# A fused diffusion layer kernel: six empty places in the order of the attention preparation, between the last tile's projections and its turned queries and keys

## The reference

```
q = (rmsnorm(q_c, qnorm_g) @ w_uq).reshape(B, L, MLA_H, QK_D)
return heads_first(with_rope(rmsnorm(q, q_g), rope))
...
k = jnp.concatenate([kv[..., :NOPE_D], broadcast(k_r)], axis=-1)
k = with_rope(rmsnorm(k, k_g), rope)
...
s = einsum('bhqd,bhkd->bhqk', q, k) * scale
o = einsum('bhqk,bhkd->bhqd', softmax(s), v)
```

## Time and profile before

| what | value |
|---|---|
| median of 3 runs | 1157.05 us (1155.04 to 1159.86) |
| the profiled execution's own time | 1148.31 us |
| its span in the profile | 1146.6 us |
| TensorE busy | 974.9 us, 85% of the span |
| VectorE busy | 451.5 us, 39% |
| ScalarE busy | 272.4 us, 24% |
| share of the chain that ended last | PE 73%, DVE 12%, issue 5% |

### The profile page before, as it was taken

How to read it: one execution, slowest core, us unless ns; L and a number is a source line. 1 busy time by engine, 2 the same in 40 slices (tenths; PEclk the granted TensorE clock), 3 DMA queues, 4 the chain that set the end, 5 groups by cost and what they waited for, 6 DMA issues and landing times.

```text
span 1146.6 us, 12445 instructions
## 1 busy us (share of the span) xinstructions
PE 974.9 (85%) x4417; PEld 537.2 (47%) x4417; DVE 451.5 (39%) x1149; ACT 272.4 (24%) x645; POOL 168.8 (15%) x204
## 2 busy tenths in 40 slices
PE   2799989979799995999999918998999698668872
PEld 0355444645476443755454404745655463433320
DVE  0305653667864245112121252266467732311103
ACT  0301213435443103021111111121436321111100
POOL 3350110201100001211212016002012000102000
PEclk8899989989999997999999968999899899889987
DMA  8962212577300009358888741522485033389973
GB/s 266 325 162 70 78 69 74 187 254 275 93 1 1 0 3 394 109 195 328 318 319 316 256 168 37 178 74 73 147 281 161 1 147 129 129 345 415 417 320 141
DMA packets 68442, 208.11 MB, mean 182 GB/s; under 512 B 10163, under 2 KB 18599, under 8 KB 59164
## 3 DMA queue, kind: packets, MB, share of 16 engines
q1 hardware_dynamic: 56416, 181.51, 42.9%
q0 software_dynamic: 9040, 16.25, 4.8%
q10 hardware_dynamic: 2924, 9.53, 2.2%
HBM read 199.99 MB, written 18.69 MB: 191 GB/s over the span
## 4 chain that ended last, share of the span: by engine, by line
PE 73%; DVE 12%; issue 5%; DMA 4%; POOL 2%; ACT 2%; ACTq 1%; SPq 0%; DVEq 0%; POOLq 0%
PE bank L1783 15%; PE bank L1701 8%; PE bank L1501 8%; PE bank L1489 8%; PE bank L1807 7%; PE bank L1411 7%; PE bank L1642 3%; PE bank L1575 3%; PE bank L1458 3%; POOL ST L1044 2%; PE bank L1553 2%; PE bank L1663 2%; PE bank L1759 2%; DMA BRANCH<-in_w_mod 1%; PE bank L1561 1%
## 5 line engine op out<-in xcount | busy, mean ns | idle before, releaser
L1783 PE MATMUL bank<-RINGW,NA 128*128 128x512 f32 (+1 forms) x448 | 176.9, 625 | 25.6 <-issue 23.2
L1783 PEld LDWEIGHTS bank<-RINGW,NA 128*128 128x128 f32 (+1 forms) x448 | 69.1, 174 | 126.4 <-issue 126.4
L1044 POOL TENSOR_TENSOR ST<-ST,RT 128x1 f32<-128x1 f32 (+4 forms) x46 | 51.4, 1117 | 502.3 <-DVE ST L1911 233.8
L1501 PE MATMUL bank<-RINGW,H 128*128 128x512 f32 (+4 forms) x384 | 119.0, 470 | 0.0
L2398 DVE SCALAR_TENSOR_TENSOR BRANCH<-BRANCH,bank 128x256 f32<-128x256 f32 x24 | 10.1, 421 | 237.9 <-ACT BRANCH L1355 237.9
L1489 PE MATMUL bank<-H,RINGW 128*96 128x512 f32 (+1 forms) x256 | 98.6, 543 | 4.0 <-ACT H L1158 2.7
L1701 PE MATMUL bank<-RINGW,H 128*128 128x512 f32 (+1 forms) x216 | 93.6, 593 | 0.0
L1501 PEld LDWEIGHTS bank<-RINGW,H 128*128 128x128 f32 x384 | 68.7, 190 | 49.4 <-issue 45.6
L1489 PEld LDWEIGHTS bank<-H,RINGW 128*96 128x96 f32 x256 | 41.6, 165 | 56.7 <-issue 51.9
L1701 PEld LDWEIGHTS bank<-RINGW,H 128*128 128x128 f32 (+1 forms) x216 | 40.6, 190 | 50.1 <-issue 50.0
L1411 PE MATMUL bank<-IDENT,WORK 128*128 128x128 f32 (+1 forms) x244 | 34.7, 291 | 34.3 <-DVE WORK L1913 33.2
(11 more groups left out here) (280 smaller groups left out, 1414.0 us busy)
## 6 DMA issues: line engine op xcount, KB each, us to landing
RINGW<-in_moe_w SPq DMA_DIRECT2D x56, 1024.0 KB, 11.3
RINGW<-in_w_mod SPq DMA_DIRECT2D x23, 2048.0 KB, 8.2
W2R<-in_moe_w SPq DMA_DIRECT2D x15, 1024.0 KB, 5.4
PROJ<-in_moe_w SPq DMA_DIRECT2D x11, 1024.0 KB, 16.8
WORK<-in_moe_w SPq DMA_DIRECT2D x8, 1024.0 KB, 18.6
RINGW<-in_w_in SPq DMA_DIRECT2D x4, 1536.0 KB, 8.3
RINGW<-in_w_out SPq DMA_DIRECT2D x4, 1536.0 KB, 10.7
RINGW<-in_w_in SPq DMA_DIRECT2D x2, 2048.0 KB, 9.4
```

The costliest lines, as they stand in the source:

```text
L1044: pool.tensor_tensor(r[:, 0:w], m[:, 0:w], POOL_HALF[:, 0:w], ALU.pow).then_inc(rstd_ready, 1)
L1501: ins = pe.matmul(bank_of(s)[:, 0:nn], HT[:, kk, t * P:(t + 1) * P], wv[:, kk, off:off + nn], start=kk == 0, stop=kk == KD - 1)
L1783: ins = pe.matmul(bank_of(s)[seats, :], XGT[n % 2][:, kk, seats], w[:, kk, :], start=kk == 0, stop=kk == KD - 1)
```

## The change

`prep` is given six entries `None` behind `uqn` of the last tile and ahead of its `qkT`. `merge` counts them as entries, so that units are set between them; then they are dropped. No step is added or removed, and no step's instructions change.

```
         prep = []
+        hold = [None] * 6
         for t in range(T + 1):
             now, last = t < T, t > 0
             prep += ([("cT", l, t)] if now else []) + ([("uqn", l, t - 1)] if last else [])
-            prep += ([("uqk", l, t)] if now else []) + ([("qkT", l, t - 1)] if last else [])
+            prep += ([("uqk", l, t)] if now else hold) + ([("qkT", l, t - 1)] if last else [])
             prep += [("uqs", l, t)] if now else []
...
-        s += spread(merge(prep, unit_steps(l, 1)), fill) + unit_steps(l, 0)
+        mixed = [x for x in merge(prep, unit_steps(l, 1)) if x]
+        s += spread(mixed, fill) + unit_steps(l, 0)
```

## The result

The changed kernel is slower: a median of 1163.82 us over 20 runs (1158.4 to 1168.74), against 1159.54 us for the kernel before over 20 runs on the same chips. The ratio is 1.0057, with a 95% interval of 1.0034 to 1.0081; it goes by the fast runs, without the three of the kernel before that lie over 1.5% above its fastest (1165.95, 1166.3 and 1376.84), and with only the last of them left out the means would give 1.0049. On the 1157.05 us of before that is +6.6 us, with an interval of +3.9 to +9.4. I had forecast +2.0 us and, with a chance of 0.62, a change too small to tell. The measured median lies inside the forecast range; the size of the change, which I had put at a third of what it is, is what failed, and in layer 1 a step of the mechanism with it.

What follows compares the result with a forecast made beforehand. TensorE, busy 85% of the span, was taken to bound the kernel, its late waits set by VectorE's in-order chain. Layer 0's -0.9 and layer 1's +2.9 us, added to 1157.05, gave 1159.0 us, range 1152 to 1166.

Steps and rivals of the forecast that it cites:

- What bounds the stage, and where the wait goes: Both layers: VectorE's in-order chain sets the end; waits move behind `uqn` 3, 2.9 us in layer 0, about 6 in layer 1.
- Layer 0, "-0.9 us": Layer 0: `uqn` 3 starts 4.5 us earlier, mostly spent on later waits; first scores at 319.5 against 320.43.
- the walk: Both layers: step-by-step timing of the new order on each engine, from measured durations and estimates for short steps.
- my bounds of -5.6 and +2.5: Layer 0: -5.6 us if the full 4.5 and 1.1 of clock come through, +2.5 if the clock is low at the end.
- Layer 1, "`uqn` 2 starts at 888.2, 0.8 us later": Layer 1: `qkT` 1, `mod` and `modT` ahead of `uqs` 2 on VectorE delay `uqn` 2 from 887.41 to 888.2 us.
- From `uqn` 2 to `uqn` 3, and from there to the scores: Layer 1: 11.4 to 12.5 us between them, before 12.3; `uqn` 3 ends 904.6 to 905.6, scores at 911.1 (909.0 to 912.2).
- The sum, "+2.0 us": Both layers: -0.9 and +2.9 us, total 1159.0 us, bounds -4.8 and +8.0; nothing behind the stages gives it back.
- less than 0.5% can't be told from no change: Whole kernel: a measurement can't resolve under 5.8 us; chances faster 0.14, within 0.62, slower 0.24.
- earlier preparation starves TensorE throughout: Rival, both layers: each `uqn` delays scores and `OM`s whose banks TensorE needs; three more waits, 9.8 us, 1167; chance 0.20.
- the places do what they seem to: Rival, both layers: both long waits vanish, as TensorE has more work beside `uqn` 3; -12.2 us, 1145; chance 0.14.
- The clock and transposes: Layer 0's tail: if transposes don't count as clock activity, some 2 us more, sum about +4; no chance changed.

Runs made afterwards that it cites:

- e4: Changed kernel with work TensorE needs (layer 0: reciprocal, `PV`, `OM`, two `S`; layer 1: `OM`, reciprocal) queued ahead of `uqn` 3; 1.0016 of the kernel before.
- e9: Kernel before plus, in layer 0 only, six places, reciprocals, `OM` and two scores ahead of `uqn` 3, `qkT` 3 and last `PV` behind four score tiles; ratio 0.9978.
- e1: Changed kernel with the six empty places in layer 0 only, layer 1 in the order of before; 1.0019 of the kernel before.
- e6: Changed kernel with matmuls nobody reads added in TensorE's long waits of both layers; 1.0028 of the kernel before.
- e3: Changed kernel with layer 1's two `mod` steps put back ahead of `uqk` 1 and `uqk` 2; 1.0087 of the kernel before.

## Why the prediction was off, point by point

- **What bounds the stage, and where the wait goes.** Right. The wait ahead of `qkT` 3 went in both layers. In layer 0 a wait for a reciprocal ahead of the `PV` sums came in its place (3.58 us, 2.9 forecast), in layer 1 a wait for an `OM` ahead of the last `PV` (6.42 us, about 6 forecast). e4 and e9 show that this queue behind `uqn` 3 is the cause: with it mended, the same places turn layer 0's loss of 1.9 us into gains of 1.8 and 4.1 us.
- **Layer 0, "-0.9 us".** The mechanism held and the term was mis-sized by 2.8 us, the larger part of the 4.2 us that the sum missed (e1 has it alone, 70.11 us against 68.25). `uqn` 3 started 54.8 us into the stage against 58.1 before, 3.3 us earlier where I had 4.5. From the end of `uqn` 3 to the first scores it was 10.4 us where I had 8.8: the walk ran the last transposes and `PV`s at full clock, and had the low one only in the bound. `ET` took 2.15 us and `PV` 1.98, both at low clock, and `qkT` 2.09, at low clock in its first part. That keeping TensorE busy there would have saved this isn't shown (e6 gained nothing in layer 0). +1.87 is within my bounds of -5.6 and +2.5.
- **Layer 1, "`uqn` 2 starts at 888.2, 0.8 us later".** This is the step whose mechanism failed. It started 3.05 us later. The walk had both long waits for `cT` and the `mod` that no longer covered them, but it had `uqk` 2 start 16.1 us into the stage and run at full clock. It started at 880.75 - 863.96 = 16.8, and the clock fell around that wait: `uqk` 2 lasted 1.8 us longer, `qkT`, `mod` and `modT` followed, and VectorE stood at `modT` for 2.95 us with `uqs` 2 behind it. I had named a low clock as a bound, and for the wrong tile (`uqk` 1, 1.5 us). e3 covers the waits, has `uqk` 2 at 2.21 us, and `uqn` 2 comes 4 us earlier. e6 leaves the order as it is, has `uqk` 2 at 2.21 us too, and `uqn` 2 comes 1.6 us earlier: that much of the 3.05 us is the clock's, the rest the order's.
- **From `uqn` 2 to `uqn` 3, and from there to the scores.** Right: 11.35 us (11.4 to 12.5 forecast), and 10.8 us from the start of `uqn` 3 to the scores (9.3 to 11.5 by my terms).
- **The sum, "+2.0 us".** Measured +6.2 in the stages and +6.6 in total; layer 0 missed by 2.8 us and layer 1 by 1.5, both towards slower. Nothing behind the stages gave it back, as said. That less than 0.5% can't be told from no change was too wide: the interval reaches 0.24% to each side. The forecast range of the total held the result because it was wide enough for both misses.
- **The rivals.** That earlier preparation starves TensorE throughout was the nearer one in kind: layer 1's new waits are such waits. But they wait for `cT`, by the loss of cover, and not for banks, and are 4.9 us (0.5 of it there before) and a clock step instead of 9.8. That the places do what they seem to didn't come true as the change stands. The layer 0 gain of e9 needs other moves as well and may be theirs alone.
- **The clock and transposes.** In the kernel before, the clock fell at 894 us during 20 transposes in a row, behind a wait of 3.27 us, and came back at 897 during value matmuls. In e9, with the same order in that layer, the same 20 transposes stayed at full clock behind a wait of 3.26 us (the last 12 in 1.47 us). Later, in e3 and e9, the low clock lasted through some 7 us of score matmuls. The Trainium skill ("TensorE: Matmul & The Clock Gate", Part 4: PE-mode transpose) says that transposes don't count as activity for the clock as other matmuls do. The fall at 894 us agrees with it; e9's 20 transposes at full clock and its low clock through the scores it doesn't explain. Layer 0's tail lost 1.6 us, near the 2 that I had put by this rule, but no run here separates the transposes from the waits.

## What to carry to other kernels

When steps are spread by number, whatever is added at one place shifts every other step, and the cover that other waits had goes with it: look for what stood in front of each wait, not only at the place that was meant to gain. Ahead of a long step in an in-order queue, put all that a faster engine will ask for while it runs (here a reciprocal, an `OM` and two score tiles, which in e4 made layer 0 3.7 us shorter than the changed kernel's). Compare such orders by stage lengths inside the trace, to the first point where the matmul clock has recovered; with the low clock in reach, an order's gain and the clock's loss are of the same size. Take more than one execution of each order: the clock alone moved one order by 3.3 us.

## What the runs showed of the hardware that I had not expected

- The clock's fall depends on more than the last wait. In the changed kernel it fell around a wait of 2.62 us that followed one of 2.32 us nine microseconds earlier, and not at one of 3.11 us (`qkT` 2 in 1.51 us). In e3 it fell at a wait of 3.12 us in the same place, and in e4, at 3.12 us too, it did not (`qkT` 2 in 1.52 us).
- Its return is as uneven. In the kernel before, the clock was back at full rate within 3 us of the start of layer 1's `qkT` 3 (904.74 us). In e9, with the same order, it was still low in the stretch to 920 us (0.56), some 10 us after that `qkT` started (909.26), and in e3 it came back some 13 us after the 5.33 us wait had ended. This moves a stage's long length by 3.3 us (71.89 and 75.15 us) with no change to its order.
